# Two pairs of weight buffers, the activations and the arena moved to other SBUF addresses

## The chip, the core and the metric

The kernel runs on one core of a Trainium2 chip. The metric is the device time of one launch in microseconds (us), as the median of several runs. The core's engines are TensorE (PE; its weight loads are listed apart as PEld), VectorE (DVE), ScalarE (ACT), GpSimd (POOL) and SyncE (SP), which here only starts transfers. SBUF is the on-chip memory that all of them read; an address below is a byte offset within one of its 128 partitions.

## The reference

Two transformer blocks follow one another on 256 tokens of width 1024, all in float32. The first has two layers, each with a feed-forward part, an attention part with three kinds of heads, and a second feed-forward part. It runs on the tokens `h` and on 256 context tokens `hc`; scales, shifts and gates come from `silu(c) @ w_ada`.

```
h = h + 0.5*g1*_swiglu(_modulate(_rms_norm(h, norm_ffn1[l]), sh1, sc1), w_ffn1_gate[l], w_ffn1_up[l], w_ffn1_down[l])
p = u @ w_in[l]                  # u: normed and modulated h
h = h + gm * (concat(y_w, y_g, y_n) @ w_out[l])   # three kinds of attention
h = h + 0.5*g2*_swiglu(...)      # second feed-forward part
```

The second block has one layer: one wide projection `h @ w_in`, three mixing branches (RWKV-7, latent attention, differential attention), gates, `merged @ w_o`, and a convolutional feed-forward part of width 2816. Nearly all arithmetic is multiplying a `[1024 or 2816] x n` weight matrix with activations of 512 columns (tokens and context) or 256 columns (tokens alone).

## The kernel before

All large weight matrices are stored in HBM as one stream of panels in the order of use. A panel is 16 tiles of 128x128 float32 (11 in the `down` stages), 1 MB. For each panel SP loads it into `raw0` or `raw1`, ACT copies it to `whi` rounded to the float32r type (line 564), DVE writes the remainder `wlo = raw - whi` (line 566), and PE multiplies. The pair `whi0`/`wlo0` serves panels of even number, `whi1`/`wlo1` those of odd number, so that one pair is filled while the other is multiplied; each of these buffers is `[P, SLAB]`, 8192 bytes in a partition. Activations are split in the same way: `u_hi`/`u_lo` (8 chunks of 512 columns), and in the arena `hidden_hi`/`hidden_lo`, `hidden_x_hi`/`hidden_x_lo`, `hid2_0`/`hid2_1`, `y_hi`/`y_lo`, `o_*_hi`/`o_*_lo`. Every product takes three matmuls (lines 1160 to 1162):

```
def three(dst, w, x, start, stop):
    pe.q.matmul(dst, w[0], x[0], start=start, stop=False)
    pe.q.matmul(dst, w[0], x[1], start=False, stop=False)
    return pe.q.matmul(dst, w[1], x[0], start=False, stop=stop)
```

`w[0]`, `w[1]` are a tile of `whi` and of `wlo`; this is the stationary operand, which PE loads with a weight load of its own before each matmul. `x[0]`, `x[1]` are the high and low part of a chunk of activations; this is the moving operand. The whole kernel has 10,944 such matmuls: 3840 on `u` with 512 columns, 3696 on `u` with 256 columns, 1776 on arena tensors with 512 columns (1584 on `hidden`, 192 on `y`), 1536 on arena tensors with 256 columns (528 on `hidden_x`, 528 on `hid2`, 192 on `y`, 288 on `o_*`), and 96 in which the weight tile is the moving operand. Close to half of each kind use pair 0 and half pair 1.

The order of the stages: `up1`, `down1`, `in` with attention, `out`, `up2`, `down2` for each of two layers, then `rwkv_in`, `diff_in`, `mla_in` and `gate_in` with the mixers between them, `branch`, `w_o`, `up_2`, `down_2`. In layer 0 all of these run with 512 columns; in layer 1 `out`, `up2` and `down2`, and everything behind them, run with 256 columns. Panels of an `up` stage hold 48 matmuls, those of a `down` stage 33. The first block's `up` stages also carry panels of `w_ada`, on which DVE works alone (line 901).

SBUF tensors are placed one behind the other in the order in which `build` asks for them, each at a multiple of 32 bytes; tensors of the arena are placed at fixed offsets from `ARENA_AT`. `mod_a` and `mod_g` (384 bytes each) are small vectors: scales and gates that DVE writes once a stage and reads as per-partition scalars.

Of the kernel before, what the change touches and what calls it, by code (L numbers as in the profile page):

```python
# [17 lines left out]
F32R = mybir.dt.float32r  # L18
# [4 lines left out]
P = 128  # L23
D = 1024
KC = D // P
# [4 lines left out]
L1 = 2  # L30
# [4 lines left out]
SLAB = KC * 2 * P  # L35
# [670 lines left out]
def build(nc, ins, out):  # L706
# [8 lines left out]
    def sb(name, shape, dt=F32):  # L715
        return nc.alloc_sbuf_tensor(name, shape, dt)
# [5 lines left out]
    vec_2 = nc.alloc_sbuf_tensor_at("vec_2", [P, VC.n - VC.kept], F32, offset=c_row_at)  # L722
    const = sb("const", [P, CC.kept])
    raw = [sb(f"raw{i}", [P, SLAB]) for i in range(2)]
    whi = [sb(f"whi{i}", [P, SLAB], F32R) for i in range(2)]
    wlo = [sb(f"wlo{i}", [P, SLAB], F32R) for i in range(2)]
    H_AT = (nc.sbuf_base + 31) // 32 * 32
    h = sb("h", [P, KC, T])
    u_hi = sb("u_hi", [P, KC, T], F32R)
# [4 lines left out]
    prod = [sb(f"prod{i}", [P, T]) for i in range(2)]  # L734
    ssq = sb("ssq", [P, T])
    mod = sb("mod", [P, 2, L1 * NMOD * KC])
    mod_a = sb("mod_a", [P, L1, 3, 2, KC])
    mod_g = sb("mod_g", [P, L1, 3, 2, KC])
    arena_size = FC * T * 4 * 2
    ARENA_AT = (nc.sbuf_base + 31) // 32 * 32  # L740
    sb("arena", [P, arena_size // 4])
# [2174 lines left out]
```

## Time and profile before

| | |
|---|---|
| median of 3 runs | 2460.35 us (2459.8 to 2464.88) |
| profiled execution, its own time | 2461.11 us |
| profiled execution, span of the trace | 2459.8 us |
| mean granted TensorE clock | 0.974 of 2.4 GHz |
| PE busy | 2319.7 us (94% of the span) |
| DVE, ACT, POOL busy | 1508.5, 966.6, 365.3 us |

The median is the number to beat. The span is the first to last instruction of the profiled execution, 1.3 us less than that execution's own time, and all durations below are taken from this one execution. PE busy is the union of its matmul records, and these overlap: a record is longer than the distance to the next one's start. So this document measures a run of matmuls by the distance between starts.

### The profile page before, as it was taken

The page shows a single profiled execution, that of the slowest core. Times are in us where ns is not written, and L with a number is a line of the kernel's source. Part 1 is how long each engine was busy: PE and PEld are TensorE (multiplying, and loading weights), DVE is VectorE, ACT ScalarE, POOL GpSimd, SP SyncE. Part 2 cuts the span into 40 slices and gives each one's busy share as a digit, 9 for nine tenths or more (in the row PEclk, how much of TensorE's full clock was granted, in tenths as well). Part 3 has the DMA queues.
Part 4 walks back from the last instruction along what each step waited for, and adds up shares of the span by engine and source line. Part 5 has one row for each costly group of instructions (what it writes and reads, how often), then busy time and mean ns, then how long its engine had stood idle before and what let it go on. Part 6 is the DMA issues. An engine that isn't in the chain of part 4 may idle for free. (4 is left out here: it accounts for less than half of the span.)

```text
span 2459.8 us, 37060 instructions
## 1 busy us (share of the span) xinstructions
PE 2319.7 (94%) x14376; PEld 1947.6 (79%) x14376; DVE 1508.5 (61%) x2305; ACT 966.6 (39%) x1538; POOL 365.3 (15%) x352
## 2 busy tenths in 40 slices
PE   6999999998999999999999989889988898998998
PEld 4888877665678888778888867579987897898998
DVE  4666666455666665576663364566668646676774
ACT  4222213455442222242222255444445234556762
POOL 1000001000000000000000010089999800000000
PEclk9999999999999999999999999989998998999999
DMA  7554444111234454434442231135452231244444
GB/s 280 189 196 163 172 152 148 67 35 52 76 139 162 162 182 149 157 128 175 180 164 94 105 108 52 54 122 184 167 174 71 103 114 52 86 155 147 171 155 144
DMA packets 52615, 331.05 MB, mean 135 GB/s; under 512 B 6544, under 2 KB 7824, under 8 KB 21648
## 3 DMA queue, kind: packets, MB, share of 16 engines
q1 hardware_dynamic: 49040, 319.15, 36.2%
q0 software_dynamic: 3456, 10.25, 1.4%
q8 instruction: 83, 1.36, 0.2%
q14 instruction: 36, 0.29, 0.0%
HBM read 325.56 MB, written 3.80 MB: 134 GB/s over the span
## 5 line engine op out<-in xcount | busy, mean ns | idle before, releaser
L1160 PE MATMUL bank<-u_hi,whi 128*128 128x512 f32 (+1 forms) x2512 | 875.8, 349 | 47.0 <-DVE wlo L566 19.0
L1161 PE MATMUL bank<-u_lo,whi 128*128 128x512 f32 (+1 forms) x2512 | 859.9, 342 | 0.0
L1162 PE MATMUL bank<-u_hi,wlo 128*128 128x512 f32 (+1 forms) x2512 | 859.4, 342 | 0.0
L566 DVE TENSOR_TENSOR wlo<-raw,whi 128x2048 fp32r<-128x2048 f32 (+2 forms) x208 | 433.8, 2085 | 287.3 <-ACT whi L564 287.1
L1160 PEld LDWEIGHTS bank<-u_hi,whi 128*128 128x128 f32 x2512 | 486.9, 194 | 124.2 <-issue 35.7
L1162 PEld LDWEIGHTS bank<-u_hi,wlo 128*128 128x128 f32 x2512 | 487.1, 194 | 51.7
L1161 PEld LDWEIGHTS bank<-u_lo,whi 128*128 128x128 f32 x2512 | 487.7, 194 | 49.7 <-issue 0.2
L564 ACT ACTIVATE whi<-raw 128x2048 fp32r<-128x2048 f32 (+2 forms) x208 | 354.5, 1704 | 158.1 <-DMA raw<-in_stream 96.8
L1222 ACT ACTIVATE sil<-bank 128x512 f32<-128x512 f32 (+1 forms) x88 | 47.9, 544 | 545.4 <-PE bank L1162 545.4
L1160 PE MATMUL bank<-hidden_hi,whi 128*128 128x512 f32 x528 | 209.5, 397 | 3.7 <-DVE wlo L566 3.7
L1162 PE MATMUL bank<-hidden_hi,wlo 128*128 128x512 f32 x528 | 208.7, 395 | 0.0
L1161 PE MATMUL bank<-hidden_lo,whi 128*128 128x512 f32 x528 | 208.7, 395 | 0.0
L1226 DVE TENSOR_TENSOR prod<-sil,bank 128x512 f32<-128x512 f32 (+1 forms) x88 | 54.7, 621 | 174.1 <-ACT sil L1222 170.5
L901 DVE SCALAR_TENSOR_TENSOR bank<-raw,c_row 128x1024 f32<-128x1024 f32 x128 | 157.2, 1228 | 2.1 <-DMA raw<-in_stream 2.1
L901 DVE SCALAR_TENSOR_TENSOR raw<-raw,bank 128x1024 f32<-128x1024 f32 x128 | 155.8, 1217 | 0.0
L587 DVE TENSOR_TENSOR wlo<-raw,whi 128x1024 fp32r<-128x1024 f32 (+2 forms) x80 | 94.6, 1195 | 91.9 <-ACT whi L579 76.3
L1330 POOL TENSOR_TENSOR rel_bias_map<-rel_bias_map,bucket_step 128x384 f32<-128x384 f32 x124 | 148.2, 1195 | 10.3
L1380 POOL DMA_DIRECT2D tables<-in_const x2 | 1.1, 572 | 981.5 <-PE bank L1162 981.5
L1327 POOL TENSOR_SCALAR bucket_step<-in_bucket,bucket_steps 128x384 f32<-128x384 f32 x124 | 139.7, 1127 | 12.5
L967 ACT ACTIVATE prod<-h 128x512 f32<-128x512 f32 (+3 forms) x63 | 33.5, 537 | 252.3 <-DVE h L1265 239.5
L1160 PEld LDWEIGHTS bank<-hidden_hi,whi 128*128 128x128 f32 x528 | 99.2, 188 | 30.3 <-DVE wlo L566 6.9
L1162 PEld LDWEIGHTS bank<-hidden_hi,wlo 128*128 128x128 f32 x528 | 99.2, 188 | 23.9
(425 smaller groups left out, 3030.8 us busy)
## 6 DMA issues: line engine op xcount, KB each, us to landing
raw<-in_stream SPq DMA_DIRECT2D x231, 1024.0 KB, 4.8
raw<-in_stream SPq DMA_DIRECT2D x80, 704.0 KB, 4.0
first_ada<-in_stream SPq DMA_DIRECT2D x8, 1024.0 KB, 17.0
raw<-in_stream SPq DMA_DIRECT2D x8, 768.0 KB, 4.3
skew<-rpb_rows POOLq DMA_DIRECT2D x8, 336.0 KB, 6.2
nbr_bias<-skew POOLq DMA_DIRECT2D x24, 112.0 KB, 3.6
h<-in_tokens SPq DMA_DIRECT2D x1, 2048.0 KB, 12.1
uq_ukv<-in_small POOLq DMA_DIRECT2D x1, 1536.0 KB, 8.0
```

Of the source, the lines that this page charges most:

```text
L564: a.activation(self.hi[to][:, 0:n], raw[:, 0:n], ACT.Copy).then_inc(self.s_hi, 1)
L566: v.tensor_tensor(self.lo[to][:, 0:n], raw[:, 0:n], self.hi[to][:, 0:n].bitcast(F32), ALU.subtract).then_inc(self.s_lo, 1)
L587: r = v.q.tensor_tensor(self.lo[to][:, cols], self.raw[slot][:, cols], self.hi[to][:, cols].bitcast(F32), ALU.subtract)
L901: r = dve.q.scalar_tensor_tensor(out=product, in0=w, scalar=1.0, in1=rows, op0=ALU.mult, op1=ALU.mult, accum_out=to)
L967: r = act.q.activation(prod[par][:, 0:n], src, ACT.Square)
L1160: pe.q.matmul(dst, w[0], x[0], start=start, stop=False)
L1161: pe.q.matmul(dst, w[0], x[1], start=False, stop=False)
L1162: return pe.q.matmul(dst, w[1], x[0], start=False, stop=stop)
L1222: act.q.activation(sil[par][:, 0:n], banks[2 * par][:, 0:n], ACT.Silu).then_inc(s_sil, 1)
L1226: dve.q.tensor_tensor(prod[par][:, 0:n], sil[par][:, 0:n], banks[2 * par + 1][:, 0:n], ALU.mult).then_inc(st.s_ev, 1)
L1327: z = pool.do(pool.q.tensor_scalar(step[:, :], bucket[:, :], 1.0 - float(start), steps[:, hh, b + 1:b + 2], ALU.add, ALU.mult))
L1330: z = pool.do(pool.q.tensor_tensor(rel[:, hh, :], rel[:, hh, :], step[:, :], ALU.add))
```

## The change

Nothing but SBUF addresses. `mod_a` and an unused gap of 64 bytes now stand between the two pairs of weight buffers, `mod_g` stands between the second pair and `h`, and a gap of 64 bytes stands ahead of the arena. The buffers are also paired differently: before, the order was `whi0 whi1 wlo0 wlo1`, now it is `whi0 wlo0 ... whi1 wlo1`.

```
-    whi = [sb(f"whi{i}", [P, SLAB], F32R) for i in range(2)]
-    wlo = [sb(f"wlo{i}", [P, SLAB], F32R) for i in range(2)]
+    whi, wlo = [None] * 2, [None] * 2
+    whi[0], wlo[0] = sb("whi0", [P, SLAB], F32R), sb("wlo0", [P, SLAB], F32R)
+    mod_a = sb("mod_a", [P, L1, 3, 2, KC])
+    sb("gap_0", [P, 16])
+    whi[1], wlo[1] = sb("whi1", [P, SLAB], F32R), sb("wlo1", [P, SLAB], F32R)
+    mod_g = sb("mod_g", [P, L1, 3, 2, KC])
     H_AT = (nc.sbuf_base + 31) // 32 * 32
     h = sb("h", [P, KC, T])
     u_hi = sb("u_hi", [P, KC, T], F32R)
...
     mod = sb("mod", [P, 2, L1 * NMOD * KC])
-    mod_a = sb("mod_a", [P, L1, 3, 2, KC])
-    mod_g = sb("mod_g", [P, L1, 3, 2, KC])
+    sb("gap_1", [P, 16])
```

The instructions of every engine, their order, waits, shapes and operands are the same in both programs. Where the tensors start, and the rest after division by 256:

| tensor | before | rest | after | rest |
|---|---|---|---|---|
| `raw0`, `raw1` | 23680, 31872 | 128 | the same | 128 |
| `whi0` | 40064 | 128 | 40064 | 128 |
| `wlo0` | 56448 | 128 | 48256 | 128 |
| `whi1` | 48256 | 128 | 56896 | 64 |
| `wlo1` | 64640 | 128 | 65088 | 64 |
| `h`, `u_hi`, `u_lo` | 72832, 89216, 105600 | 128 | 73664, 90048, 106432 | 192 |
| `sil`, `prod`, `ssq`, `mod` | 121984 and on | 128 | 832 bytes higher | 192 |
| arena (`hidden`, `y`, `o_*`, `hid2`) | 134144 | 0 | 134272 | 128 |

Every tensor that moves through PE in lines 1160 to 1162 starts, chunk by chunk, a multiple of 512 bytes behind one of these numbers or (some arena tensors) of 256, and every weight tile a multiple of 512 bytes behind its buffer's. So the distance from the weight tile to the moving chunk has one rest after division by 256 for each kind:

| moving, weights | before | after |
|---|---|---|
| `u`, pair 0 | 0 | 64 |
| `u`, pair 1 | 0 | 128 |
| arena, pair 0 | 128 | 0 |
| arena, pair 1 | 128 | 64 |

## Rows read from the trace of the kernel before

**Rows 1.** The page: busy time of each engine.

```profile
PE 2319.7 (94%) x14376; PEld 1947.6 (79%) x14376; DVE 1508.5 (61%) x2305; ACT 966.6 (39%) x1538; POOL 365.3 (15%) x352
```

**Rows 2.** Waits of PE: total, times, longest, in us.

```profile
PE bank L1160 <- DVE wlo L566: 31.6, 35, 3.2
PE bank L1160 <- DVE u_lo L1114: 13.6, 7, 2.9
```

**Rows 3.** Windows: busy us by engine, in five stages.

```profile
core 0: us, PE busy (x) PEld busy (x) DVE busy (x) ACT busy (x) POOL busy (x), PEclk, DMA share, GB/s
679.00:922.00 243.00, 242.28 (x1057) 199.95 (x1058) 164.27 (x222) 73.76 (x86) 0.00 (x0) 0.99 0.45 162
922.00:1048.00 126.00, 124.27 (x532) 99.13 (x531) 70.51 (x105) 29.00 (x28) 0.00 (x0) 1.00 0.44 154
...
1631.00:1762.00 131.00, 129.76 (x1058) 129.09 (x1059) 83.41 (x75) 59.26 (x76) 121.90 (x99) 0.98 0.46 165
1762.00:1832.00 70.00, 64.66 (x531) 63.03 (x529) 42.98 (x34) 29.75 (x35) 65.03 (x55) 1.00 0.49 171
...
2213.00:2382.00 169.00, 157.83 (x1255) 154.25 (x1256) 122.15 (x191) 114.95 (x186) 0.00 (x0) 0.97 0.44 158
```

**Rows 4.** Timeline, PE, stage up1, layer 0: start, duration, line.

```profile
100.06 0.39 PE L1162 MATMUL bank<-u_hi,wlo 128*128 128x512 f32 x1
100.29 0.39 PE L1160 MATMUL bank<-u_hi,whi 128*128 128x512 f32 x1
...
110.94 0.39 PE L1162 MATMUL bank<-u_hi,wlo 128*128 128x512 f32 x1
```

**Rows 5.** Timeline, PE, stage down1, layer 0.

```profile
330.84 0.40 PE L1160 MATMUL bank<-hidden_hi,whi 128*128 128x512 f32 x1
331.08 0.39 PE L1161 MATMUL bank<-hidden_lo,whi 128*128 128x512 f32 x1
331.31 0.40 PE L1162 MATMUL bank<-hidden_hi,wlo 128*128 128x512 f32 x1
331.55 0.39 PE L1160 MATMUL bank<-hidden_hi,whi 128*128 128x512 f32 x1
...
338.55 0.39 PE L1160 MATMUL bank<-hidden_hi,whi 128*128 128x512 f32 x1
```

**Rows 6.** Timeline, PE, stage up2, layer 1.

```profile
1649.91 0.28 PE L1160 MATMUL bank<-u_hi,whi 128*128 128x256 f32 x1
1650.03 0.28 PE L1161 MATMUL bank<-u_lo,whi 128*128 128x256 f32 x1
...
1655.67 0.28 PE L1160 MATMUL bank<-u_hi,whi 128*128 128x256 f32 x1
```

**Rows 7.** Timeline, PE, stage down2, layer 1.

```profile
1802.15 0.29 PE L1160 MATMUL bank<-hidden_x_hi,whi 128*128 128x256 f32 x1
1802.27 0.28 PE L1161 MATMUL bank<-hidden_x_lo,whi 128*128 128x256 f32 x1
...
1806.07 0.28 PE L1160 MATMUL bank<-hidden_x_hi,whi 128*128 128x256 f32 x1
```

**Rows 8.** Windows of two stretches at the lower clock.

```profile
core 0: us, PE busy (x), PEclk, DMA share, GB/s
1634.00:1636.60 2.60, 2.19 (x10) 0.50 0.00 0
41.00:42.60 1.60, 1.60 (x5) 0.50 0.95 312
```

**Rows 9.** Timeline, PE, in the second of these stretches, up1.

```profile
40.78 0.63 PE L1160 MATMUL bank<-u_hi,whi 128*128 128x512 f32 x1
41.21 0.63 PE L1161 MATMUL bank<-u_lo,whi 128*128 128x512 f32 x1
41.63 0.63 PE L1162 MATMUL bank<-u_hi,wlo 128*128 128x512 f32 x1
42.06 0.63 PE L1160 MATMUL bank<-u_hi,whi 128*128 128x512 f32 x1
```

**Rows 10.** Timeline, PE, in the first of these, up2.

```profile
1635.34 0.42 PE L1162 MATMUL bank<-u_hi,wlo 128*128 128x256 f32 x1
1635.55 0.42 PE L1160 MATMUL bank<-u_hi,whi 128*128 128x256 f32 x1
...
1636.40 0.41 PE L1161 MATMUL bank<-u_lo,whi 128*128 128x256 f32 x1
```

**Rows 11.** Groups by line, up2, layer 0: count, busy us, mean ns.

```profile
L566 DVE TENSOR_TENSOR wlo<-raw,whi 128x2048 fp32r<-128x2048 f32 x20 | 45.8, 2292 | 21.5 <-ACT whi L564 21.5
L564 ACT ACTIVATE whi<-raw 128x2048 fp32r<-128x2048 f32 x20 | 38.2, 1908 | 0.0
```

**Rows 12.** Waits in stage down2 of layer 1.

```profile
DVE wlo L566 <- ACT whi L564: 9.8, 10, 1.8
PE bank L1160 <- DVE wlo L566: 5.3, 8, 0.9
```

## The prediction

> **What bounds the kernel now.** I read first the busy times: PE is busy for 94% of the span, the next engine, DVE, for 61% [rows 1]. Then the waits of PE: the longest sum, that for the split weights, is 31.6 us in 35 waits, the next 13.6 us in 7 [rows 2]; together under 2% of the span. Then the windows by stage: in `up2` of layer 0 PE is busy 242.3 of 243 us while DVE has 164.3 and ACT 73.8; in `down2` 124.3 of 126; in `up2` of layer 1 129.8 of 131 [rows 3]. So in most of the program the end is set by how fast PE starts one matmul after the other, and the other engines have a third of their time to spare.
>
> The change alters no instruction, so it can act only through how long an instruction takes. The question is whether the addresses of the operands do that. The starts of PE's matmuls answer it.
>
> - `u` chunks, 512 columns: 48 matmuls from the start at 100.06 to that at 110.94, 10.88/48 = 226.7 ns each [rows 4].
> - `hidden` chunks, 512 columns, the same three lines and shapes: 33 from 330.84 to 338.55, 7.71/33 = 233.6 ns each; the first starts lie 0.24, 0.23 and 0.24 apart, so one in two is longer [rows 5].
> - `u`, 256 columns: 48 from 1649.91 to 1655.67, 120.0 ns each [rows 6].
> - `hidden_x`, 256 columns: 33 from 1802.15 to 1806.07, 118.8 ns each [rows 7].
> - At half the clock (1.2 GHz, granted 0.50 [rows 8]) 512 columns on `u` take 1.28/3 = 427 ns [rows 9] and 256 columns 1.06/5 = 212 ns [rows 10]: one column in each cycle and nothing over. At 2.4 GHz the same would be 213 and 107 ns.
>
> So at the full clock each matmul pays 12 to 20 ns above its columns, at half the clock nothing, and how much depends on which tensor moves: +6.9 ns for the arena at 512 columns, -1.2 ns at 256. Shape, type, weights and the order are the same; what differs is the address. This looks like PE's two streams out of SBUF, the moving chunk and the next tile's weights, getting in each other's way. The table of distances gives the only difference that I find: from weights to moving chunk it is 0 for `u` and 128 for the arena, after division by 256.
>
> **The skill against the rows.** The Trainium skill (TensorE: Matmul & The Clock Gate, Back-to-back issue gap) gives N/1.2 ns at the low clock, which agrees with 427 and 212, and N/2.4 + 2.5 ns at the high one, 216 and 109 ns, where the rows have 227 to 234 and 119 to 120. The Trainium skill (SBUF — State Buffer, Who interferes with whom) gives PE two independent read ports and says that it never waits on anyone; by that, addresses would change nothing and the sum would be 0. The difference between `u` and `hidden` speaks against it, but doesn't show that the distance is the cause.
>
> **The change, part by part.** The time is taken as decided by that distance. Half of each kind of matmul uses each pair of weight buffers.
>
> 1. Distances that the trace shows, exchanged. `u` on pair 1 goes from 0 to 128, arena on pair 0 from 128 to 0. 512 columns: 1920 x (233.6 - 226.7) = +13.2 us and 888 x -6.9 = -6.1 us. 256 columns: 1848 x -1.2 = -2.2 us and 768 x +1.2 = +0.9 us. Sum **+5.8 us**.
>
> 2. A distance that no row shows, 64: `u` on pair 0 (1920 with 512 columns, 1848 with 256) and the arena on pair 1 (888 and 768). Lower bound: the streams never meet and a matmul takes its columns alone, 213.3 and 106.7 ns: 1920 x 13.4 + 1848 x 13.3 + 888 x 20.3 + 768 x 12.1 = 25.7 + 24.6 + 18.0 + 9.3 = 77.6 us saved. Upper bound: 64 is worse than both known distances by as much as these differ, 240.5 and 121.2 ns: 1920 x 13.8 + 1848 x 1.2 + 888 x 6.9 + 768 x 2.4 = 26.5 + 2.2 + 6.1 + 1.8 = 36.6 us lost. I choose the same step downward: better than both known distances by what these differ, 219.8 and 117.6 ns. That is 1920 x 6.9 + 1848 x 1.2 + 888 x 13.8 + 768 x 1.2 = 13.2 + 2.2 + 12.3 + 0.9 = **-28.6 us**. My reason for the lower side: both known distances are whole multiples of 128, both cost about the same (13 and 20 ns over the columns), and a distance off that grid is the one thing that hasn't been seen; nothing in the rows shows a cost above 20 ns. It is a choice, not a reading.
>
> 3. ACT and DVE. Their buffers move as well: ACT writes `whi`, DVE reads `raw` and `whi` and writes `wlo`. 2048 elements take ACT 1908 ns and DVE 2292 ns [rows 11], 0.93 and 1.12 ns an element with their fixed part. Both lie behind a panel's 48 matmuls of 10.9 us; with all of DVE's work in `up2` at 164.3 of 243 us [rows 3] either could be a third slower before PE waited. I cost this at nothing. Without that cover, 5% on DVE's 208 splits would be 0.05 x 208 x 2.3 = 24 us.
>
> 4. Scales, gates and gaps. `mod_a` and `mod_g` are read as one scalar per partition, and the gaps by nobody: 0. Loads into `raw` go to the addresses of before: 0.
>
> 5. What PE can't keep. In `down2` of layer 1 PE waits 5.3 us in 8 waits for `wlo`, and DVE itself waits 9.8 us for ACT [rows 12], which may only fill `whi` once the panel before last is multiplied. There a shorter matmul makes that wait longer: PE is busy 64.7 of 70 us, and the 264 matmuls on pair 1 would give 0.3 us by item 2, 3 us at its bound. So this changes little in the likeliest case. In the 169 us of `up_2` PE is busy 157.8 [rows 3], and a gain of 1% there mostly arrives.
>
> Sum: 5.8 - 28.6 = -22.8 us. The 96 matmuls with the weight tile moving can't add more than 96 x 13 ns = 1.2 us, and I leave them out. The profiled execution took 2461.1 us, 0.8 us above the median of 2460.35, so the sum gives 2438.3 us against it and 2437.6 us against the median. I say **2439 us** for the little that waits take back.
>
> **The rivals.**
>
> A. The floor. At 64 the two streams miss each other altogether: 5.8 - 77.6 = -71.8 us, 2389 us. For it: at half the clock PE does run at exactly one column a cycle [rows 9, 10]. Against: that is with twice the time for each access, and 107 ns a matmul would leave `up2` of layer 1 less than 5.2 us a panel, near to where other waits begin.
>
> B. The other side: 64 is a bad distance. Where the moving chunk and the weights are half as far out of step as at 128, each pass may cost more than at either. At the upper bound of item 2 that is 5.8 + 36.6 = +42 us, 2503 us; with 64 at the arena's cost of today, 233.6 and 118.8 ns, it is 5.8 + 13.2 - 2.2 = +17 us, 2477 us. The point that decides: 5424 matmuls go to 64, so they must each be 5.8/5424 = 1.1 ns shorter than today for the change to break even. For it: the exchange in item 1 is already a loss, and alternating starts in the arena rows [rows 5] show that these costs jump rather than glide. The weak place of my forecast is here.
>
> C. The change doesn't act. `u` and the arena differ in more than the distance: the arena lies above 134144, `u` below 122000. If it is the region that costs 6.9 ns, both tensors keep theirs, and the time stays 2460 us. The Trainium skill (SBUF — State Buffer, Who interferes with whom) would give the same time, by its two independent ports. For a region: `y`, `hidden`, `hid2` are all in that region. Against: a region can't make 512 columns slower and 256 faster, while two streams that meet at other moments could.
>
> D. It is the moving chunk's own rest that counts, not the distance. Then the arena goes from 0 to 128, `u`'s rest of today: 1776 x -6.9 + 1536 x 1.2 = -10.4 us, while `u` goes to 192, unseen, at between -12 and +14 ns a matmul of 512. This gives either sign; I spread it over the others.
>
> **How the numbers follow.** A change of 0.2% (5 us) is about what a measurement of this kernel can tell from none. Forecast (faster, 2415 to 2455): 0.36. A: 0.16. B: 0.32. C: 0.16. Faster 0.52, same 0.16, slower 0.32. The range reaches from 2395, near A's floor, to 2490, between B's two figures, and leaves out some 0.1 on each side. The likeliest case alone has 2415 to 2455.
>
> **What would show it.** Starts of PE's matmuls on pair 0 and on pair 1, which today are equal, must part: on `u` with 512 columns about 220 against 234 ns, in `down1` about 227 on pair 0 against 220 on pair 1. `up2` of layer 0 would have 227 ns a matmul on average over both pairs and stay near 243 us, and the `down` stages would gain most, 126 to about 120 us. More than 227 ns on pair 0 with `u` shows B; four unchanged figures show C; equal pairs with other figures show D. ACT's 1908 and DVE's 2292 ns should stay. What would make the prediction wrong above all is the guess of the cost at 64, on which all of the -28.6 us rests.

## The result and the profile after

The changed kernel takes 2472.45 us (2470.29 to 2473.67, 6 runs) against 2461.93 us before (2459.80 to 2464.88, 6 runs): 1.0038 times before's, 95% interval 1.0027 to 1.0049. It is slower by some 10 us, where 23 less were forecast. The profiled execution spans 2471.0 us, 11.2 more than before's.

The page's first lines, which answer to [rows 1]: PE's busy time has grown by 0.8 us only, DVE, ACT and POOL stand where they were.

```profile
span 2471.0 us, 37060 instructions
PE 2320.5 (94%) x14376; PEld 1940.4 (79%) x14376; DVE 1507.4 (61%) x2305; ACT 966.5 (39%) x1538; POOL 364.3 (15%) x352
```

The distance between PE's starts tells more. The timeline of PE at the end of `up1` of layer 1, one panel on pair 1 and then one on pair 0, each from its first to its last of 48 matmuls (47 distances; [rows 4] before):

```profile
1288.95 0.39 PE L1163 MATMUL bank<-u_hi,whi 128*128 128x512 f32 x1
...
1299.92 0.39 PE L1165 MATMUL bank<-u_hi,wlo 128*128 128x512 f32 x1
1300.15 0.39 PE L1163 MATMUL bank<-u_hi,whi 128*128 128x512 f32 x1
...
1310.90 0.40 PE L1165 MATMUL bank<-u_hi,wlo 128*128 128x512 f32 x1
```

Pair 1, now at distance 128: 10.97/47 = 233.4 ns. Pair 0, now at 64: 10.75/47 = 228.7 ns. Both had 226.7. Next, the first panel of `down1` of layer 1, on pair 1 at distance 64, 32 distances ([rows 5] before, 233.6 ns):

```profile
1311.14 0.39 PE L1163 MATMUL bank<-hidden_hi,whi 128*128 128x512 f32 x1
...
1318.46 0.40 PE L1165 MATMUL bank<-hidden_hi,wlo 128*128 128x512 f32 x1
```

7.32/32 = 228.8 ns. In `up2` of layer 1, first a panel on pair 1, then one on pair 0 ([rows 6] before, 120.0 ns):

```profile
1652.07 0.27 PE L1163 MATMUL bank<-u_hi,whi 128*128 128x256 f32 x1
...
1657.64 0.28 PE L1165 MATMUL bank<-u_hi,wlo 128*128 128x256 f32 x1
...
1737.40 0.28 PE L1163 MATMUL bank<-u_hi,whi 128*128 128x256 f32 x1
...
1742.94 0.29 PE L1165 MATMUL bank<-u_hi,wlo 128*128 128x256 f32 x1
```

5.57/47 = 118.5 and 5.54/47 = 117.9 ns. And in `down_2`, 256 columns from the arena on pair 0 (distance 0) and on pair 1 (64):

```profile
2395.80 0.28 PE L1163 MATMUL bank<-hid,whi 128*128 128x256 f32 x1
...
2399.64 0.28 PE L1165 MATMUL bank<-hid,wlo 128*128 128x256 f32 x1
...
2453.49 0.28 PE L1163 MATMUL bank<-hid,whi 128*128 128x256 f32 x1
...
2457.11 0.28 PE L1165 MATMUL bank<-hid,wlo 128*128 128x256 f32 x1
```

3.84/32 = 120.0 and 3.62/32 = 113.1 ns.

Over all matmuls at the full clock, without those that wait, the mean distances of starts in the two traces are:

| kind (number) | before | after, pair 0 | after, pair 1 |
|---|---|---|---|
| `u`, 512 columns (3840) | 227.1 ns at distance 0 | 229.1 at 64 | 232.9 at 128 |
| `hidden`, 512 columns (1584) | 233.2 at 128 | 227.1 at 0 | 229.2 at 64 |
| `u`, 256 columns (3696) | 119.8 at 0 | 117.5 at 64 | 118.7 at 128 |
| `hidden_x`, `hid2`, `o_*`, 256 columns (1344) | 118.7 at 128 | 119.8 at 0 | 115.5 at 64 |

The times of the stages, from the start of a stage's first of these matmuls to that of its last, read from the same timelines:

| stage | before | after | difference, us |
|---|---|---|---|
| `up1` layer 0, `up2` layer 0, `up1` layer 1 | 243.0, 242.1, 242.1 | 247.5, 246.4, 246.4 | +13.1 |
| `down1` and `down2` layer 0 | 125.7, 125.5 | 125.7, 125.9 | +0.4 |
| `down1` layer 1 | 123.0 | 120.1 | -2.9 |
| `up2` layer 1 | 130.3 | 128.6 | -1.7 |
| `down2` layer 1 | 70.0 | 70.8 | +0.8 |
| `up_2` | 169.4 | 169.1 | -0.3 |
| `down_2` | 67.9 | 69.6 | +1.7 |

These sum to +11.1 us, the whole difference of the spans. The three `up` stages lose what the distances say. The two `down` stages of layer 0 gain nothing, although their matmuls are 4 to 6 ns shorter. The window on `down2` of layer 0, that on `down1` of layer 1 and that on `up2` of layer 1 (busy us of PE, PEld, DVE, ACT, POOL, as in [rows 3]):

```profile
931.00:1057.00 126.00, 121.91 (x532) 98.76 (x531) 70.63 (x105) 28.90 (x29) 0.00 (x0) 1.00 0.44 152
1311.00:1432.00 121.00, 121.00 (x536) 99.81 (x535) 40.48 (x50) 29.31 (x29) 0.11 (x1) 1.00 0.31 101
1643.00:1771.00 128.00, 127.06 (x1054) 126.33 (x1054) 83.31 (x74) 59.19 (x75) 119.26 (x96) 0.98 0.48 167
```

In the first PE is busy 121.9 of 126 us, where it had 124.3 of 126: it now waits. In the second it is busy throughout, and that stage is 2.9 us shorter.

### The profile page after: what moved, and what is told of

It is laid out like the page before. It is cut to its first block and busy times, and to the rows that moved or that the text cites. A ratio compares the mean times of both kernels' runs of the same rounds, so it can differ in the third digit from the quotient of the medians.

```text
span 2471.0 us, 37060 instructions
## 1 busy us (share of the span) xinstructions
PE 2320.5 (94%) x14376; PEld 1940.4 (79%) x14376; DVE 1507.4 (61%) x2305; ACT 966.5 (39%) x1538; POOL 364.3 (15%) x352
## 5 line engine op out<-in xcount | busy, mean ns | idle before, releaser
L1164 PE MATMUL bank<-u_lo,whi 128*128 128x512 f32 (+1 forms) x2512 | 860.3, 342 | 0.0
L1164 PEld LDWEIGHTS bank<-u_lo,whi 128*128 128x128 f32 x2512 | 483.0, 192 | 55.0 <-issue 0.2
L1164 PE MATMUL bank<-hidden_lo,whi 128*128 128x512 f32 x528 | 206.6, 391 | 0.0
L1330 POOL TENSOR_SCALAR bucket_step<-in_bucket,bucket_steps 128x384 f32<-128x384 f32 x124 | 136.3, 1099 | 12.5
L1163 PEld LDWEIGHTS bank<-hidden_hi,whi 128*128 128x128 f32 x528 | 99.1, 188 | 34.0 <-DVE wlo L566 12.5
```

The lines of the kernel that those rows point to most:

```text
L1330: z = pool.do(pool.q.tensor_scalar(step[:, :], bucket[:, :], 1.0 - float(start), steps[:, hh, b + 1:b + 2], ALU.add, ALU.mult))
```

## The experiments

**all_64: everything moved, distances kept.** Does an operand's own address count?

```
+    sb("gap_r", [P, 16])
     raw = [sb(f"raw{i}", [P, SLAB]) for i in range(2)]
```

> One gap of 64 bytes ahead of the raw buffers, so that raw, the weight pairs, u and the arena all lie 64 bytes higher. Every distance from weights to moving chunk stays as before (u 0, arena 128), every tensor's own rest changes. If the distance alone decides: 226.7 ns a matmul on u with 512 columns, 233 on hidden, 120 and 118.6 with 256 columns, and a time within 0.2% of before. If a tensor's own address counts, at least one of the four moves by over 1 ns.

Measured: 0.9996 times before's (0.9987 to 1.0005). One panel on `u` and one on `hidden`:

```profile
890.88 0.39 PE L1161 MATMUL bank<-u_hi,whi 128*128 128x512 f32 x1
...
901.54 0.39 PE L1163 MATMUL bank<-u_hi,wlo 128*128 128x512 f32 x1
...
1307.21 0.39 PE L1161 MATMUL bank<-hidden_hi,whi 128*128 128x512 f32 x1
...
1314.68 0.39 PE L1163 MATMUL bank<-hidden_hi,wlo 128*128 128x512 f32 x1
```

10.66/47 = 226.8 and 7.47/32 = 233.4 ns, as before. With 256 columns the means are 119.8 and 118.7. Addresses of their own, moved together by 64 bytes, don't count, whereas the changed kernel gave the two weight pairs different costs on one and the same `u`. The distance decides.

**arena_0: the arena alone, distance 0.**

```
+    sb("gap_2", [P, 32])
     arena_size = FC * T * 4 * 2
```

> One gap of 128 bytes ahead of the arena: arena distance 0 on both pairs, u untouched at 0. By distance: hidden 226.9 ns (before 233), arena with 256 columns 119.8 ns (before 118.6). Theory 'the down stages that also carry w_ada panels are paced by a chain of loads and splits and not by PE': the first two down stages stay near 125.7 us and only down1 of layer 1 falls, from 123 to 120; sum with out about -4 us, +1 us for 256 columns, so 2458 us. Rival 'the matmuls pace all of them': 1776 x 6.3 = -11 us, +1.5 us, so 2452 us.

Measured: 2455.9 us, 0.9967 of before (0.9955 to 0.9979), faster by some 8 us. `hidden` has 226.9 ns, arena matmuls with 256 columns 119.9. The stages: `down1` and `down2` of layer 0 stay at 125.4 us each, `down1` of layer 1 falls from 123.0 to 119.5. The window on `down2` of layer 0 and that on `down1` of layer 1:

```profile
922.00:1047.00 125.00, 120.68 (x527) 98.26 (x526) 70.16 (x105) 28.74 (x28) 0.00 (x0) 1.00 0.44 154
1297.00:1417.00 120.00, 120.00 (x531) 99.41 (x530) 40.10 (x49) 28.99 (x28) 0.00 (x0) 1.00 0.29 100
```

And PE's waits in the first of these windows:

```profile
PEld bank L1161 <- DVE wlo L566: 6.4, 5, 1.7
PE bank L1161 <- DVE wlo L566: 4.3, 5, 1.2
```

So the first theory holds where it can be read off: two of the three stages keep 0.3 and 0.1 of 528 x 6.3 = 3.3 us. The whole time wouldn't have decided it: it fell by twice the 4 us that this theory gave and lies nearer to the rival's 10. Of the 5.3 us between the two spans the three `down` stages give 3.9. What paces them is seen in the timeline of that stage, matmuls left out (`DVE L902` is DVE's work on a `w_ada` panel, line 901 before; the last two lines are from the next such round):

```profile
945.63 1.38 ACT L564 ACTIVATE whi<-raw 128x1408 fp32r<-128x1408 f32 x1 [6.00 <-DMA raw<-in_stream]
...
947.05 1.63 DVE L566 TENSOR_TENSOR wlo<-raw,whi 128x1408 fp32r<-128x1408 f32 x1 [5.75 <-ACT whi L564]
...
948.59 1.23 DVE L902 SCALAR_TENSOR_TENSOR bank<-raw,c_row 128x1024 f32<-128x1024 f32 x1
...
953.17 0.87 DVE L1266 SCALAR_TENSOR_TENSOR h<-bank,mod_g,h 128x256 f32 x2
...
954.24 0.63 ACT L968 ACTIVATE prod<-h 128x512 f32 x1 [7.23 <-DVE h L1266]
...
954.78 1.37 ACT L564 ACTIVATE whi<-raw 128x1408 fp32r<-128x1408 f32 x1
...
956.18 1.63 DVE L566 TENSOR_TENSOR wlo<-raw,whi 128x1408 fp32r<-128x1408 f32 x1 [0.49 <-ACT whi L564]
...
972.63 1.62 DVE L566 TENSOR_TENSOR wlo<-raw,whi 128x1408 fp32r<-128x1408 f32 x1 [0.58 <-ACT whi L564]
...
974.31 0.50 PE L1161 MATMUL bank<-hidden_hi,whi 128*128 128x512 f32 x1 [0.29 <-DVE wlo L566]
```

DVE's products stand for 4.6 us (948.59 to 953.17) ahead of the update of `h`; ACT's square and, behind it in ACT's queue, the next panel's `whi` wait for that update; then comes `wlo`. In this round it ends at 957.8, still 1.1 us before PE takes up that panel at 958.89. But one round of two panels takes the chain 16.4 us (`wlo` ends at 957.8 and at 974.25), and PE only 66 x 226.8 ns = 15.0 us, so that from the next round on PE stands and waits: it starts at 974.31. DVE is busy 56% of the stage and is still late: it is one queue in which a long block stands ahead of a short step that others wait for.

**before_narrow and arena_0_narrow: DVE's block made short.** For every `w_ada` panel behind the first eight these leave out three quarters of the sums that make the scales and gates, so their output isn't that of the reference; they serve only to time the rest.

```
-            w = raw[slot][:, c * D:(c + 1) * D]
-            for s, (rows, product) in enumerate(((c_row[:, :], unread), (c_ctx_psum, w))):
+            w = raw[slot][:, c * D:c * D + 256]
+            for s, (rows, product) in enumerate(((c_row[:, 0:256], unread[:, 0:256]), (c_ctx_psum[:, 0:256], w))):
```

> The kernel before, but DVE's four products for each w_ada panel behind the first eight take 256 columns instead of 1024; the rest of those sums is left out. Theory 'the down stages with w_ada panels are paced by DVE's queue': down1 and down2 of layer 0 go from 125.7 us to what the matmuls need, 528 x 233.2 = 123.1 us. Rival 'they are paced by loads or by the matmuls': they stay at 125.7. The up stages, bound by the matmuls, keep 242 to 243 us. So 2457 us or 2462.

> arena_0 with the same 256-column products. Theory of DVE's queue: the first two down stages go from 125.4 to 528 x 226.8 = 119.8 us, 11 us less than arena_0, 2445 us, so that the gain of the matmuls, lost in arena_0, arrives here. Rival of loads or matmuls: they stay at 125.4 and the time at 2456 us.

Measured: 2452.8 us, 0.9962 (0.9947 to 0.9976), and 2440.2 us, 0.9921 (0.9895 to 0.9947). The window on `down2` of layer 0 in each:

```profile
918.00:1041.00 123.00, 123.00 (x529) 98.96 (x528) 49.72 (x105) 29.02 (x28) 0.00 (x0) 1.00 0.43 151
```

```profile
912.00:1032.00 120.00, 120.00 (x532) 99.34 (x531) 49.72 (x105) 29.20 (x28) 0.00 (x0) 1.00 0.44 155
```

PE is busy without a gap in both, and all three `down` stages with 512 columns take 123.0 us in the one, 119.5 us in the other. So the arena's distance gains 3.9 us in the three `down` stages beside the full products and 10.5 us beside the narrow ones. The whole times agree, 8 and 10 us by the ratios (12.5 by the medians of the narrow pair), but their intervals are too wide to show it alone. Of the 6.1 us between the spans of before and before_narrow (2459.8 and 2453.7) the two stages of layer 0 make 5.2. DVE's queue was late by that much in the kernel before already, behind the longer matmuls.

**after_narrow: the change with the short block.**

> The changed kernel with the 256-column w_ada products of before_narrow. If the whole loss of the change is what the three up stages with 512 columns lose while DVE's queue keeps back what the down stages gain, then here the down stages fall to 528 x 228 = 120.3 us each, three times 2.7 us less than in before_narrow (123.0), the up stages keep their +4.4 us each, and the time comes to 2452.8 + 13.2 - 8.1 - 1.7 - 0.5 = 2456 us, only 3 us above before_narrow, where the change itself costs 10 us. If the loss has another source, it stays 10 us above before_narrow, at 2463 us.

Measured: 2458.7 us, 0.9980 of before (0.9970 to 0.9989). Window on `down2` of layer 0:

```profile
924.00:1044.50 120.50, 120.50 (x531) 99.33 (x530) 49.71 (x105) 28.99 (x28) 0.00 (x0) 1.00 0.45 154
```

All three `down` stages take 120.1 us, the `up` stages 247.5, 246.4, 246.4. Against before_narrow's 0.9962 the change costs 0.18%, some 4 us (spans 2457.4 and 2453.7), where against before it costs 0.38%; 3 us were expected, 10 by the rival. With the intervals of both ratios these 4 us are good to about 4, so the stages must speak: the two `down` stages of layer 0 are 5.8 us shorter than in before_narrow, while in the changed kernel they are 0.4 us longer than before. So about half of the measured loss was gain kept back by DVE's queue.

**both_64, both_192, both_32: other distances for both kinds on both pairs.** both_64 and both_32 add a gap ahead of `h` and one ahead of the arena; both_192 has `mod_a` (taken from its place ahead of the arena) and a gap of 64 bytes ahead of `h`, and no gap ahead of the arena.

```
     wlo = [sb(f"wlo{i}", [P, SLAB], F32R) for i in range(2)]
+    sb("gap_1", [P, 16])                                   # both_64; both_32: [P, 8]
...
+    sb("gap_2", [P, 32])                                   # not in both_192
```

> Distance 64 for u and the arena on both pairs. By distance: u and hidden with 512 columns 229.1 ns, u with 256 columns 117.5 ns, arena with 256 columns 115 to 116 ns. Against before +2.4 x 3840 = +9 us, -2.4 x 3696 = -9 us of which a part is taken back by waits, and little in the down stages: 2460 to 2464 us. If instead the two pairs had to differ for these costs, the figures per pair will not be those of the changed kernel.

> Distance 192 for u and the arena on both pairs, the one class of 64 bytes that neither kernel has in its large stages. Only 43 matmuls with the weight tile moving had it, at 114.8 ns with 256 columns. If it costs what 64 costs (distance counted without sign): 229.1, 117.5 ns and the time of both_64. If it is the class in which the streams miss each other: 216 to 224 ns and 113 to 115 ns, 3840 x 5 + 3696 x 5 = up to -38 us, 2425 to 2450 us.

> Distance 32 for u and the arena, both pairs. If the cost depends on which 64-byte piece both are in, this costs what 0 costs (227.0 and 119.8 ns, time of arena_0, 2456 us). If it glides, it lies between 0 and 64: 228 and 118.6 ns, 2459 us. If a start inside a 64-byte piece costs something of its own, 512 columns take over 233 ns and the time is over 2475 us.

Measured: both_64 2464.5 us, 1.0000 (0.9991 to 1.0009); both_192 2476.0 us, 1.0061 (1.0047 to 1.0074); both_32 2480.9 us, 1.0074 (1.0051 to 1.0097). A panel of each with 512 columns on `u`, and for both_192 also one with 256; both_64:

```profile
751.15 0.39 PE L1162 MATMUL bank<-u_hi,whi 128*128 128x512 f32 x1
...
761.91 0.39 PE L1164 MATMUL bank<-u_hi,wlo 128*128 128x512 f32 x1
```

both_192:

```profile
859.48 0.39 PE L1161 MATMUL bank<-u_hi,whi 128*128 128x512 f32 x1
...
870.45 0.39 PE L1163 MATMUL bank<-u_hi,wlo 128*128 128x512 f32 x1
...
1733.11 0.28 PE L1161 MATMUL bank<-u_hi,whi 128*128 128x256 f32 x1
...
1738.44 0.28 PE L1163 MATMUL bank<-u_hi,wlo 128*128 128x256 f32 x1
```

both_32:

```profile
199.56 0.40 PE L1162 MATMUL bank<-u_hi,whi 128*128 128x512 f32 x1
...
210.53 0.39 PE L1164 MATMUL bank<-u_hi,wlo 128*128 128x512 f32 x1
```

That is 10.76/47 = 228.9, 10.97/47 = 233.4 and 5.33/47 = 113.4, and 10.97/47 = 233.4 ns. So 192 isn't 64 without its sign, nor does it leave the streams free with 512 columns, which I had given it as the hopeful case; with 256 columns it gives the shortest matmuls. 32 neither equals 0 nor lies between 0 and 64 with 512 columns: of the three cases expected for it, the third came (over 233 ns, over 2475 us). For both_64 the time and both figures on `u` held (229.1 and 117.5 ns), and `hidden` had 229.2 ns. Arena matmuls with 256 columns had 117.2, not 115 to 116 ns.

**wlo_64: only `wlo` moved.**

```
     whi = [sb(f"whi{i}", [P, SLAB], F32R) for i in range(2)]
+    sb("gap_0", [P, 16])
     wlo = [sb(f"wlo{i}", [P, SLAB], F32R) for i in range(2)]
+    mod_a = sb("mod_a", [P, L1, 3, 2, KC])
+    sb("gap_1", [P, 16])
...
-    mod_a = sb("mod_a", [P, L1, 3, 2, KC])
```

> Only the wlo pair lies 64 bytes higher than whi, u and the arena stay at distance 0 from whi; from wlo both are at 192. While line 1160 streams u_hi the next weights loaded are whi (distance 0), while 1161 streams u_lo they are wlo (192), while 1162 streams u_hi they are whi (0). Theory 'the moving chunk meets the weights loaded for the next matmul': on u with 512 columns 1161 takes 233 ns, 1160 and 1162 take 227, mean 229. Rival 'it meets its own weights': 1162 takes 233 and the other two 227. Rival 'the start of a matmul carries the delay of the one before': the long one is one line later. Total near before's: +2.1 x 3840 = +8 us on u with 512 columns, -1.5 x 3696 = -5.5 us with 256.

Measured: 2471.2 us, 1.0049 (1.0036 to 1.0062), some 12 us longer where +8 - 5.5 us had been expected. PE's starts in `up1` of layer 0:

```profile
86.04 0.40 PE L1164 MATMUL bank<-u_hi,wlo 128*128 128x512 f32 x1
86.28 0.39 PE L1162 MATMUL bank<-u_hi,whi 128*128 128x512 f32 x1
86.50 0.39 PE L1163 MATMUL bank<-u_lo,whi 128*128 128x512 f32 x1
86.73 0.40 PE L1164 MATMUL bank<-u_hi,wlo 128*128 128x512 f32 x1
86.97 0.39 PE L1162 MATMUL bank<-u_hi,whi 128*128 128x512 f32 x1
```

From each start of L1164 (line 1162 before, `u_hi` with `wlo`) it is 0.24 us to the next start, from the others 0.22 and 0.23; over all of them 235.3, 228.6 and 229.4 ns. The long one is the matmul whose own weights are at 192, or it carries over the delay of the one before: these two can't be told apart by this run. The first theory in its plain form, that the matmul streaming while `wlo` is loaded is itself the long one, has fallen; with the delay carried over by one start it would stand. The mean, 231.1 ns, is no mixture of 227 and 233 in the ratio 2 to 1 either, which would be 229. So a matmul's cost isn't set by its own distance alone; it depends on its neighbours' too.

**best: 512 columns at 0, 256 columns at 192.** From arena_0; `norm` and the products of `up2` of layer 1 and of `up_2` get

```
+    u_off = (u_hi[:, :, 48:48 + S], u_lo[:, :, 48:48 + S])
```

> arena_0, and in up2 of layer 1 and in up_2 the activations stand 48 elements (192 bytes) further in their chunk, so that 256 columns run at distance 192 while 512 columns stay at 0. By the costs per distance: up2 of layer 1 falls from 130.3 to 126.8 us, up_2 by 1 us, the rest as in arena_0: 4 to 5 us under it, 0.5% under before, near 2450 us. If the cost of a distance were one for the whole kernel and not for the operand, 512 columns would change too.

Measured: 2449.3 us, 0.9949 of before (0.9932 to 0.9967), faster than both kernels of this case. `up2` of layer 1, window:

```profile
1629.00:1754.50 125.50, 124.49 (x1056) 123.43 (x1057) 83.35 (x74) 59.19 (x75) 117.04 (x93) 0.98 0.48 172
```

A panel of `up1` of layer 1 (512 columns) and one of `up2` of layer 1 (256):

```profile
1266.39 0.39 PE L1162 MATMUL bank<-u_hi,whi 128*128 128x512 f32 x1
...
1277.04 0.39 PE L1164 MATMUL bank<-u_hi,wlo 128*128 128x512 f32 x1
...
1638.52 0.28 PE L1162 MATMUL bank<-u_hi,whi 128*128 128x256 f32 x1
...
1643.85 0.28 PE L1164 MATMUL bank<-u_hi,wlo 128*128 128x256 f32 x1
```

10.65/47 = 226.6 and 5.33/47 = 113.4 ns. `up2` of layer 1 takes 125.4 us instead of arena_0's 130.3, `up_2` 166.3 instead of 168.7; 126.8 us and 1 us less had been expected.

## Why the prediction was wrong

- **Addresses decide through the distance from weights to moving chunk: right**, in the form in which it was told. The changed kernel exchanged the costs of 0 and 128 between `u` and the arena, and all_64 kept every cost with all addresses moved. Rivals C (a region, or nothing) and D (the chunk's own rest) fell with these. What stays an inference is the picture behind it, of two streams that meet in SBUF: the runs show that the distance decides, not how.
- **Item 1, distances exchanged: right.** +5.8 us was forecast; by the measured means 1920 x 5.8 (`u`, pair 1) - 888 x 6.1 - 1848 x 1.1 + 768 x 1.1 = 11.1 - 5.4 - 2.0 + 0.8 = +4.5 us.
- **Item 2, the unseen distance 64: this step failed.** It said "better than both known distances by what these differ", 219.8 and 117.6 ns. 256 columns came to 117.5 on `u`, 115.5 in the arena. 512 columns came to 229.1 ns, between the two known, so that `u` on pair 0 lost 2.0 ns a matmul, +3.8 us, instead of gaining 6.9. The item was forecast at -28.6 us; the measured means give 1920 x 2.0 - 888 x 4.0 - 1848 x 2.3 - 768 x 3.2 = -6.4 us, so that 22 of the 34 us between forecast and result are this term. The reason given, that 64 lies off the grid of 128, was a choice from two known costs, as the text said; rival A, its extreme form with 213 and 107 ns, fell with it.
- **Item 5, what PE can't keep: this term was too small, and it turned the sign.** By the measured costs the sum would be 4.5 - 6.4 = -1.9 us, and the spans say +11.2. Most of the 13.1 us between them are gains that didn't arrive. Some 5.7 us lie in the two `down` stages of layer 0, which by the means should be shorter by 528 x 6.1 + 528 x 4.0 = 5.3 us and are 0.4 longer: I had read 124.3 us busy in a window of 126 [rows 3] as bound by PE and by nothing else, though DVE's queue stood a hair behind. The matmuls with 256 columns should have given 7.9 us. `up2` of layer 1 kept all of its part, 1.7 us, but `up_2`, of which the text said that a gain there mostly arrives, kept 0.3 of 2, and `down2` of layer 1 [rows 12] and `down_2` came out 0.8 and 1.7 us longer. For `down_2` the clock has most of it: behind a wait of PE of 2.7 us, 14 of its matmuls ran at 1.2 GHz, at 213 instead of 118 ns, 1.3 us, where before had none. after_narrow, with the same addresses and the same wait, had none either and took 68.2 us there, so this part need not come from the change. Against all this stand some 2 us that the sum counts as lost with 512 columns and that the three `up` stages don't show.
- **Items 3 and 4: right.** DVE's and ACT's busy times are the same to 1.1 and 0.1 us.
- **Rival B** had the sign, and by the sign that the prediction set for it (over 227 ns on pair 0 with `u`) it came: 228.7 ns. But neither of its figures did: 64 is not worse than both known distances, nor as costly as the arena's today, and it is luck that its +17 us lies near the measured 11: about half of these are gains that DVE's queue kept back, which no rival had. The break-even that it was given, 1.1 ns for each of the 5424 matmuls, took for granted that all gains arrive. The range, 2395 to 2490, held the time.
- The Trainium skill (TensorE: Matmul & The Clock Gate, Back-to-back issue gap) gives N/2.4 + 2.5 ns for a matmul by itself at the full clock, an estimate of 216 and 109 ns; no distance tried here reached either with these float32r matmuls and a weight load ahead of each, the shortest settled figures being 226.7 and 113.3. The Trainium skill (SBUF — State Buffer, Who interferes with whom) has PE wait on nobody; against other engines nothing here speaks against that, but the costs of PE's own two streams, whose ports the page calls independent, depend on where their operands stand to each other, by up to 6.7 ns in 227. Here the measurement decides.

What stays open: the rule behind the costs per distance, why the chain in `up_2` takes back nearly all that its matmuls gain, and whether a matmul pays for its own weights or for the delay of the one before.

## What to carry to other kernels

Measure the distance between the starts of consecutive matmuls, in one long run for each kind of operand, and compare it with columns over clock: a surplus that differs between operands of one shape is a matter of their addresses, and a gap of 32 to 128 bytes changes it in either direction. A cost seen at two distances says nothing of a third; each has to be measured. Before a faster engine is counted, look for the engine that is just barely hidden behind it: a gap-free PE in one stage and 1% of waiting in the next are not the same, and a queue with a long block ahead of a short needed step keeps the gain for itself at 56% busy.

## What the runs showed of the hardware

The costs of a matmul with a weight load of its own, float32r, 128x128 weights, settled runs at 2.4 GHz:

| distance, rest after division by 256 | 512 columns, ns | 256 columns, ns |
|---|---|---|
| 0 | 226.7 | 120.0 |
| 32 | 233.3 | 116.7 |
| 64 | 228.9 | 117.8, in some panels 113.3 |
| 128 | 233.3 | 118.6 |
| 192 | 233.3 | 117.8, in some panels 113.3 |

At 1.2 GHz it was 427 ns [rows 9] and 212 ns [rows 10], without a surplus, and not at distance 0 alone: over the matmuls on `u` with 512 columns at that clock, both_192 and both_32 have means of 426.7 and 426.6 ns. At 2.4 GHz, 226.7 and 233.3 ns are 32 and 48 cycles over the 512 columns, and 113.3, 116.7 and 120.0 ns are 16, 24 and 32 over the 256, worked out from these figures. The order of the distances is not the same at 512 and at 256 columns, so no one placement is best for both. At 64 and 192 with 256 columns one and the same code runs at either of two figures. In `up2` of layer 1 in both_192 the figure settles in the first few matmuls behind a wait of PE and then holds, over several panels, until PE waits again: 117.8 ns for 286 matmuls, then 113.3 ns for 334. The rest 64 was run at 64 and at 320 bytes in 512 (arena on pair 1 and `u` on pair 0 of the changed kernel), with the same 229 ns, and 192 at 192 (best) and 448, with the same two figures; 0 and 128 were run only at 0 and 384, so for these the division by 256 is assumed.
